# One encoder layer on one core: value and recurrence-input projections moved ahead of the head groups and made token-major, groups cut from 12 to 10 tiles

## The reference

```python
xn = rmsnorm(x, norm_pre_w)
h = xn @ w_in                                   # 2048 x 13312
na_q, na_k, na_v, na_z, hg_q, hg_ff, hg_fb, hg_i, hg_z, gate_pre = split(h)
o_a = neighbourhood_attention(na_q, na_k, na_v, bias) * silu(na_z)      # 16 heads of 64
f, key = lb + (1 - lb) * sigmoid(f_pre), (1 - lb) * sigmoid(-f_pre)     # per direction
# recurrence, forward and backward, 8 heads of 128:
#   S_t = diag(f_t) S_{t-1} + key_t outer i_t ;  o_t = S_t^T q_t
o_b = rmsnorm(o_fwd + o_bwd, hg_norm_w) * silu(hg_z)
g_a, g_b = split(sigmoid(gate_pre + b_gate))
y = g_a * (o_a @ w_branch[:1024]) + g_b * (o_b @ w_branch[1024:])
out = x + rmsnorm(y @ w_out, norm_post_w)
```

## Time and profile before

| | us |
|---|---|
| median of 3 runs | 861.09 (859.41 to 861.10) |
| profiled execution, its own time | 860.94 |
| its span, first to last instruction | 859.2 |
| PE busy | 841.3 (98%) |
| DVE busy | 636.9 (74%) |
| ACT busy | 404.2 (47%) |
| POOL busy | 46.6 (5%) |
| DMA, all queues | 153.44 MB, mean 179 GB/s |

### The profile page before, as it was taken

The page is one execution under the profiler, slowest core; times in us unless marked ns, Lnnn a source line. Parts: engine busy times, 40 slices in busy tenths (PEclk is TensorE's granted clock), DMA queues, the critical chain, the costliest instruction groups (busy, mean ns, idle before and its releaser), DMA issues.

```text
span 859.2 us, 14528 instructions
## 1 busy us (share of the span) xinstructions
PE 841.3 (98%) x4913; PEld 730.7 (85%) x4913; DVE 636.9 (74%) x1304; ACT 404.2 (47%) x667; POOL 46.6 (5%) x51
## 2 busy tenths in 40 slices
PE   6999999999999999999999999999999999999995
PEld 5888888888888888888888888888888888888884
DVE  4877876886888688688878868876875777774444
ACT  6554444435444453644544454345444555554442
POOL 5300000000100000010000001000000000000002
PEclk9999999999999999999999999999999999999998
DMA  9967658565675766666566666656566866576522
GB/s 287 239 183 190 170 148 206 154 191 151 169 191 147 180 180 165 177 164 176 162 167 183 160 181 157 172 164 175 157 186 165 226 185 178 180 275 213 190 100 99
DMA packets 270966, 153.44 MB, mean 179 GB/s; under 512 B 15240, under 2 KB 261088, under 8 KB 270304
## 3 DMA queue, kind: packets, MB, share of 16 engines
q1 hardware_dynamic: 269936, 149.17, 63.5%
q10 hardware_dynamic: 1008, 3.98, 1.2%
HBM read 151.04 MB, written 2.10 MB: 178 GB/s over the span
## 4 chain that ended last, share of the span: by engine, by line
PE 96%; DMA 1%; DVE 1%; ACT 1%; POOL 0%; DVEq 0%; issue 0%; SPq 0%; ACTq 0%
PE psum L960 52%; PE psum L962 26%; PE psum L1034 3%; PE psum L1155 3%; PE psum L1157 3%; PE psum L1156 3%; DMA raw<-in_w_in 1%; PE psum L1020 1%; PE psum L1009 1%; PE psum L989 1%; PE psum L1047 1%; PE psum L1039 0%; PE psum L998 0%; PE psum L1054 0%; ACT w_hi L387 0%; DVE big L922 0%
## 5 line engine op out<-in xcount | busy, mean ns | idle before, releaser
L960 PE MATMUL psum<-act_hl,w_hi 128*128 128x512 f32 x1664 | 593.2, 400 | 0.0
L962 PE MATMUL psum<-act_hl,w_lo 128*128 128x256 f32 x1664 | 463.9, 279 | 0.0
L597 DVE TENSOR_TENSOR w_lo<-raw,w_hi 128x1024 fp32r<-128x1024 f32 x270 | 328.0, 1254 | 75.6 <-ACT w_hi L387 75.1
L960 PEld LDWEIGHTS psum<-act_hl,w_hi 128*128 128x128 f32 x1664 | 312.3, 188 | 73.2 <-DVE w_lo L597 3.1
L962 PEld LDWEIGHTS psum<-act_hl,w_lo 128*128 128x128 f32 x1664 | 313.7, 189 | 0.0
L387 ACT ACTIVATE w_hi<-raw 128x1024 fp32r<-128x1024 f32 x272 | 272.8, 1051 | 30.8 <-PE psum L1157 25.7
L398 ACT ACTIVATE part<-psum 128x256 f32<-128x256 f32 x104 | 39.6, 381 | 261.1 <-PE psum L962 261.1
L960 PE MATMUL psum<-branch_hl,w_hi 128*128 128x512 f32 x256 | 90.7, 399 | 0.0
L962 PE MATMUL psum<-branch_hl,w_lo 128*128 128x256 f32 x256 | 71.9, 281 | 0.0
L960 PEld LDWEIGHTS psum<-branch_hl,w_hi 128*128 128x128 f32 x256 | 48.1, 188 | 12.2 <-DVE branch_hl L763 0.3
L657 DVE TENSOR_TENSOR hg<-hg 128x128 f32<-128x128 f32 x224 | 50.7, 288 | 0.3
(11 more groups left out here) (124 smaller groups left out, 543.3 us busy)
## 6 DMA issues: line engine op xcount, KB each, us to landing
raw<-in_w_in SPq DMA_DIRECT2D x104, 1024.0 KB, 5.7
raw<-in_w_branch SPq DMA_DIRECT2D x16, 1024.0 KB, 6.0
raw<-in_w_out SPq DMA_DIRECT2D x16, 1024.0 KB, 5.1
bias_t<-in_na_rel_bias SPq DMA_DIRECT2D x32, 96.0 KB, 5.7
big<-in_x SPq DMA_DIRECT2D x2, 1024.0 KB, 6.3
big<-in_x ACTq DMA_DIRECT2D x2, 1024.0 KB, 6.8
out<-big SPq DMA_DIRECT2D x5, 256.0 KB, 2.7
wide<-in_norm_post_w ACTq DMA_DIRECT2D x1, 1024.0 KB, 4.7
```

What stands on the lines that cost most here:

```text
L597: nc.vector.tensor_tensor(w_lo[:, i, :], raw[:, r, 1024 * h:1024 * (h + 1)], w_hi[:, i, :].bitcast(F32), ALU.subtract).then_inc(lo_ready, 1)
L960: nc.tensor.matmul(sums[h][:, :], w_hi[:, i, w], operand[:, k, :], start=first, stop=False, skip_group_check=True)
L962: ins = nc.tensor.matmul(sums[h][:, 0:T], w_lo[:, i, w], operand[:, k, 0:T], start=False, stop=last, skip_group_check=True)
```

## The change

1. Value (v) and recurrence input (i) of all heads leave the groups. They are projected first, in 16 tiles of the token-major shape of stage 4 (`early_tile`), 4 blocks of 4 tiles, from x that is transposed unscaled. The result of a block is scaled by the root mean square when ACT copies it out (`take_block`) to the places in `big` that gates take later. Groups have 10 slots; no transposes of v and i; ACT copies v and i of a group to `v_now` and `i_now`.
2. x is loaded in column halves, the weight tiles 0 and 1 between them, tile 0 in two halves. The warm-up matmuls no longer wait for x; there are 12 instead of 16.
3. The scaled `act_hl` is made beside tiles 6 to 14: DVE adds the parts of x and multiplies by the scale (`scale_pair`), ACT makes the high part (`act_hi`), DVE the low part (`act_lo`).
4. The four multiplications of `grow` and of `decayed` become two each, on 256 columns, with an address pattern that goes from one side's tile to the other's and back (`sides`).
5. Steps of a group have other slots; the loop's body is two groups. `hgrn_sum` writes its own bank.
6. At the end DVE weighs the output sums in PSUM in place, and the last scaling reads PSUM instead of SBUF.

```diff
-IN_SLOTS = 12
+IN_SLOTS = 10
+PRE_BLOCKS = 4
+N_PRE = 4 * PRE_BLOCKS
-WARM_UP = 16
+WARM_UP = 12
...
+            load_x(0)
+            early(0)
+            early(1)
+            load_x(1)
+            for n in range(2, N_PRE):
+                early(n)
...
+            for h in range(2):
+                x_hi(2 * h)
+                x_hi(2 * h + 1)
+                split_hi(0, 0, 0, h)
+            for k in range(4, 8):
+                x_hi(k)
+            split_tile(*early_place(1))
+            square(0)
+            for h in range(2):
+                split_hi(*early_place(2), h)
+                x_hi(8 + 2 * h)
+                x_hi(9 + 2 * h)
+            for k in range(12, 16):
+                x_hi(k)
+            square(1)
+            for n in range(2, N_PRE):
+                split_tile(*early_place(n + 1))
+                if n % 4 == 0:
+                    take_block(n // 4 - 1)
...
+                if 6 <= n < 14:
+                    act_hi(n - 6)
...
             def grow(half):
-                for i, (dst, side, src) in enumerate((
-                        (suf_f, 0, bc(pre_f, 1, half - 1)), (pre_b, 1, bc(suf_b, 0, 0)),
-                        (pre_f, 1, bc(pre_f, 0, half - 1)), (suf_b, 0, bc(suf_b, 1, 0)))):
...
+                hg_s.done(nc.vector.tensor_tensor(sides(suf_f, pre_b, half), sides(suf_f, pre_b, half),
+                                                  sides(pre_f, suf_b, half, 2 * half - 1, 0, 0), ALU.mult))
+                hg_s.settle(dve)
+                hg_s.done(nc.vector.tensor_tensor(sides(suf_b, pre_f, half), sides(suf_b, pre_f, half),
+                                                  sides(suf_b, pre_f, half, half, half - 1, 0), ALU.mult))
...
+                if 7 <= n < 15:
+                    act_lo(n - 7)
+                if 6 <= n < 14:
+                    scale_pair(n - 6)
...
-                nc.vector.tensor_tensor(block_columns(o_tok[:, t, :], c), at(psum, c * 2 + t),
+                nc.vector.tensor_tensor(at(psum, c * 2 + t), at(psum, c * 2 + t),
...
+            def early_tile(n):
+
+                c, r = n // 4, n % 4
+                for h in range(2):
+                    if (n, h) == (1, 1):
+                        turn_x(1)
...
+                    if c == 0:
+                        pe.wait_ge(xn_ready, 4 * r + 2 * h + 2)
+                    elif c > 1 and r == 0 and h == 0:
+                        pe.wait_ge(block_taken, 2 * (c - 1))
+                    pe.wait_ge(lo_ready, n * 2 + h + 1)
+                    i = (2 * r + h) % HALVES
                     for t in range(2):
+                        sums = bank[4 + 2 * (c % 2) + t]
+                        for kk in range(2):
...
+                            nc.tensor.matmul(sums, hi, w_hi[:, i, w], start=(k == 0), stop=False)
+                            nc.tensor.matmul(sums, hi, w_lo[:, i, w], start=False, stop=False)
+                            ins = nc.tensor.matmul(sums, lo, w_hi[:, i, w], start=False, stop=(k == KT - 1))
+                    ins.then_inc(half_used, 1)
```

More of the change, by code:

```diff
@@ L157, in encoder_layer @@
         ps_heads = (ps_s, ps_pt)
-        turn_bank = bank[5:8] + bank[0:4] + bank[5:6]
+        turn_bank = bank[0:4] + bank[6:8] + bank[0:2]
+        rstd_rows = ps_o
+        x_hl = branch_hl
+        squares = [hg[:, 4 + 4 * t:8 + 4 * t, :].rearrange("p a b -> p (a b)") for t in range(2)]
+        turner = hg[:, 12, :].rearrange("p (t c) -> p t c", t=2)
+        x_pair = (hg[:, 0:2, :], hg[:, 2:4, :])
+        first_landed = [sem(f"first_landed{h}") for h in range(2)]
         raw_landed = [sem(f"raw_landed{i}") for i in range(RAW)]
@@ L236, in column @@
             return ap[:, i:i + 1] if isinstance(i, int) else ap[:, bass.ds(i, 1)]
-        def pairs(ap, half):
-            return ap.rearrange("p (n two h) -> p n two h", two=2, h=half)
         def both_tiles(ap):
@@ L282, in _ @@
+            load_x(0)
[4 more added lines that the diff above has]
+                early(n)
+            for p in range(2):
+                group(0, p)
+            with loop(sp, 2, NG - 1, 2) as g0:
+                for p in range(2):
+                    group(g0, p)
             for t in range(TAIL):
-                col = GATE_TILE + 3 * NG + t
-                load(t % RAW, w_in_v[:, :, col * P:col * P + P], tile_no(NG, t))
+                col = GATE_TILE + TAIL_GATES[t]
+                n, r, _ = place(NG, 0, t)
+                load(r, w_in_v[:, :, col * P:col * P + P], n)
@@ L513, in _ @@
+            group(0, 0, True)
+            group(0, 1, False)
+            with loop(act, 2, NG - 1, 2) as g0:
+                for p in range(2):
+                    group(g0, p, False)
             for t in range(TAIL):
-                n = tile_no(NG, t)
-                split_next(n, n // RAW, n % RAW)
+                split_tile(*place(NG, 0, t + 1))
                 if t > 0:
-                    gate_tanh(3 * NG + t - 1, n - 1)
+                    gate_tanh(TAIL_GATES[t - 1], NG, t - 1)
@@ new lines, in rstd_set_up, with make_turner @@
+            def rstd_set_up():
+                dve.wait_ge(ss_ready, 4)
+                link(nc.vector.tensor_tensor(ssum, ssq[:, 0:2], ssq[:, 2:4], ALU.add))
+                nc.vector.tensor_scalar(msq, ssum, 1.0 / D, EPS, ALU.mult, ALU.add).then_inc(msq_ready, 1)
+            def make_turner():
+                dve.wait_ge(rstd_ready, 1)
+                dve.wait_ge(const_step, 5)
+                for t in range(2):
+                    nc.vector.tensor_scalar(turner[:, t, :], block[:, 0, :], rstd[:, t:t + 1], None,
+                                            ALU.mult).then_inc(turner_ready, 1)
@@ L856, in _ @@
+            group(0, 0, True)
+            group(0, 1, False)
+            with loop(dve, 2, NG - 1, 2) as g0:
+                for p in range(2):
+                    group(g0, p, False)
             for t in range(TAIL):
-                n = tile_no(NG, t)
-                split_next(n, n % RAW)
+                split_tile(*place(NG, 0, t + 1)[0:2])
                 previous(NG, t)
-                take_tile(n, t % 2, gates[:, 3 * NG + t, :])
+                take_tile(NG, t, gates[:, TAIL_GATES[t], :])
@@ L1091, in previous, with group @@
                     turn_rst(g - 1)
-            def group(g, first):
+            def group(g0, p, first):
+                g = g0 + p
                 for s in range(IN_SLOTS):
-                    n = tile_no(g, s)
-                    wait(pe, tile_out, n - 1)
+                    n, r, _ = place(g0, p, s)
+                    wait(pe, tile_out, made(g, s - 2))
                     def between():
```

499 lines of the change are left out of this document (269 added, 230 removed).

## The result

The changed kernel takes 854.0 us (median of 4 runs, 853.1 to 856.2) against 860.9 of before (859.4 to 861.1): ratio 0.9927, 95% interval 0.9915 to 0.994. That is 0.7% faster, where 1.5% was forecast. Forecast and time are 6.2 us apart. The profiled execution is the slowest of the four, 856.16 us for a span of 854.4; the others have spans of 851.4 to 852.3. The sum of the prediction was 846.1 of span, so 8.3 us of that trace have to be found.

The account below looks back on a forecast made before the run. PE was taken to bound the kernel. From a span of 859.2, 7.6 us (early stage), 3.7 (transposes of v and i) and 1.8 (end) leave 846.1; plus 1.74 outside the span, 847.8 us, range 844.5 to 856.

Parts of the forecast that it names:

- the start: Before the early tiles: vectors there by 5.9 us, first projection matmul at 10.4, 6.2 us earlier than before.
- The chain behind the vectors: Before the early tiles: first bank full at 7.1 us, ACT's copies and both halves, then first matmul at 10.4.
- the pace after it: First early tiles: matmuls as fast as the same form in the output projection, 227 ns each.
- rival (a): Early stage gives most gain back: late vectors or slow PE pace (2.2 us), the circle 2.5 more; 850 to 854, chance 0.22.
- the circle: Tiles 6 to 15: ACT and DVE wait on each other, 6.1 us a turn against PE's 5.44; PE waits 1.2 us.
- the form: Sixteen early tiles: token-major takes 5.44 us a tile against 5.655 feature-major, 3.4 us less in all.
- Groups: Groups of 10 tiles instead of 12: 64.2 us of PE instead of 76.0, nothing added to the path.
- i's transposes: In the groups: taken at 0.23 us like v's; dropping both saves 3.7 us in all.
- 5.655 us of a tile: Pitch of a feature-major tile, two of which were subtracted from each group's 76.0 us.
- DVE had room: In the groups: DVE busy 51.1 of 64.2 us, with 30 merged level operations at 0.36 each.
- Rival (b): DVE bounds the groups; merged operations at 0.68 us would make 868 us, deciding from about 0.65 a piece; chance 0.10.
- The end: After the last matmul: DVE's three additions take 2.1 us instead of 4.08; 1.8 us less for the whole.

Follow-up runs that it names:

- e11: Changed kernel with all of SP's loads held back until the four vector loads have landed: 856.0 us, one run.
- e12: Changed kernel with x's left halves loaded at once but the weights held back until the four vector loads have landed: 855.5 us, one run.
- e2: Changed kernel with x's left half transposed ahead of the small vectors: 852.1 us, ratio 0.9903 to the kernel before.
- e9: As e7, but 24 warm-up pieces instead of 36 and 28 filler pieces instead of 30: 849.1 us, ratio 0.9877 to the kernel before.
- e1: Changed kernel with 22 warm-up matmuls instead of 12 and 14 unread ones after x's first transposes: 852.5 us, ratio 0.9909 to the kernel before.
- e6: Changed kernel with the old unmerged `grow` and `decayed`, eight operations in place of four: 854.6 us, ratio 0.9925 to the kernel before.
- e8: Changed kernel run once more, unchanged: 854.2 us, ratio 0.9929 to the kernel before.
- e4: Changed kernel with the recurrence level put ahead of the heads' outputs in slot 7: 854.1 us, ratio 0.9931 to the kernel before.
- e5: Kernel before with only part 6 of the change (output sums weighed in PSUM, last scaling reads PSUM): 859.9 us, ratio 0.9988.
- e7: Changed kernel with x transposed first, 36 warm-up pieces, 30 filler pieces, and e3's order: 850.8 us, ratio 0.989 to the kernel before.
- e3: Changed kernel with DVE's multiplication by the scale ahead of the next tile's low halves: 852.2 us, ratio 0.9913 to the kernel before.
- e10: e7's kernel again, unchanged, beside e9: 851.4 us, ratio 0.9901 to the kernel before.

## Why the prediction was half right

**Wrong: the start.** The step that failed is "The vectors (norm weights) must be there by 5.9 too"; of the last of them it says itself that "the trace doesn't show when it lands". From it the first matmul was put at 10.4. In the changed kernel they land at 8.2, behind the traffic (e11, e12). The trace of before does date them, against that sentence: the last 26 of the 144 packets of their queue pass between 7 and 8 us there (none between 8 and 9), so they landed at 7 to 8 us. That queue in the kernel before, from 7 to 8 us (packets, MB, share of the engines):

```profile
q10 hardware_dynamic: 26, 0.00, 2.2%
```

The chain behind the vectors was forecast rightly: from the first full bank to the first matmul 3.3 us in the sum (7.1 to 10.4), and from ACT's first copy on 3.2 in the trace (10.11 to 13.29). With x transposed first (e2, e9) what remains of this error is 12.1 against 10.4, 1.7 us.

**Wrong: the pace after it.** "Its cost could differ only if the early matmuls were slower than the same form in the output projection, and I know no reason for it". The reason was named in rival (a) and priced at 2.2; it came to 2.9 (e1). It was argued away with one pause of 1.4 us in the earlier trace rows behind which the transposes ran at full pace. Here PE had two pauses, 2.06 and 2.01 us, and the granted clock read 0.50 from 10 to 18 us. The argument went from one pause to a rule. Rival (a), 850 to 854 us with a chance of 0.22, is what happened, at its upper edge, by both halves of its first condition (late vectors and the slow pace); its other part, 2.5 us more from the circle, did not.

**Right: the form.** 24 matmuls take 5.44 us in the early tiles too: behind the slow stretch they follow each other by 0.23 (21.01, 21.24, 21.47 in the timeline), and nothing but the slow stretch and the one wait is added. e9's tile 16, 89.35 us after its first matmul, is 16 x 5.44 = 87.0, 1.84 and 0.36 for transposes, and 0.1.

**The circle: right in its turn, lucky in its wait.** 6.1 us a turn were forecast and 5.93 measured; the lead at the start of the circle was 4.3 us forecast and 4.2 measured. By that a tile loses 0.5 and not 0.7, and the lead lasts: without the mask beside the multiplication PE does not wait (e6, e8). The wait of 1.1 us in this trace against 1.2 forecast is luck, since it needs 1.7 us of DVE beside POOL's mask, which the sum did not have.

**Groups: a tile's price was mis-sized.** The group is 64.38 us instead of 64.2, with PE never waiting for DVE. It is not the level operations (e6) and not the weight load behind the heads' outputs (e4). Nor is it i's transposes, taken by analogy with v's at 0.23: in before the level's matmuls start 0.22 behind them. It is the 5.655 us of a tile, read in the branch projection and used for tiles of the groups. In the groups 16 pairs of matmuls take mostly 16 x 0.3467 = 5.55 us; over the whole group of before, in which about a quarter of the pairs go at 0.353, it is 5.57. In the timeline of before, 30 pairs without a step between them, and i's transposes:

```profile
195.85 0.40 PE L960 MATMUL psum<-act_hl,w_hi 128*128 128x512 f32 x1
...
206.25 0.40 PE L960 MATMUL psum<-act_hl,w_hi 128*128 128x512 f32 x1
...
226.81 0.38 PE L998 MATMUL psum<-block,hg 128*128 128x128 f32 x2
227.03 0.61 PE L1034 MATMUL psum<-q_dec,k_dec 128*128 128x128 f32 x4
```

With it a group is 76.0 - 2 x 5.57 - 2 x 0.22 = 64.42, and 15 tiles at 0.085 less make 1.3 of the 1.7 us. The other 0.4 stay open.

DVE had room, as forecast: 53.90 busy of 64.38 instead of 51.1, of which 30 merged operations at 0.42 instead of 0.36 are 1.8. Rival (b), 868 us, needed 0.65 a piece. By the Trainium skill (Vector Engine (DVE) Microarchitecture Reference, 5.2 Measured stream behaviour on trn2) an operation whose tiles alternate at every word costs about twice the usual time an element (0.58 us in the prediction's estimate), and those with longer runs nothing more. The trace agrees within a tenth: L738's seven in that group have a mean of 449 ns with a median of 419 and a highest of 632, so one of the seven takes 0.63. With L741's highest, 646, and the products of level 0 at 0.49 it is 0.6 us a group, against an estimate of 0.8. All of it is hidden.

**The end.** 1.8 forecast, 1.1 measured (e5 alone 1.1 too). DVE's three additions are 2.07, forecast at 2.1, and the last addition, now POOL's (2.93 went to 2.49), ends 2.0 us nearer to the last matmul. The term that was missing is the outputs behind the additions: the sum left their time as it was, and it rose by 1.0 us (e5).

**The profile and the runs.** 854.4 of span is the longest of the four executions. How long the slow stretch lasts varies: 13 slow matmuls in this trace, 7 in e8's of the same kernel, which has no wait at tile 15 either. The size of the error by the runs is 6.2 us.

## What to carry to other kernels

When loads are moved ahead or reordered, give each small one that gates the start a landing time of its own; issued at 2 us beside megabytes of other traffic, it may land at 8. Where the start is made of short waits of PE, fill them with matmuls nobody reads (e1, and e9 against the changed kernel), but no longer than the wait, since every piece too many delays what is ready (e7 against e9). At the end of a kernel, sum up to the last output and not to the last operation: additions that ended 2.0 us earlier brought the end 1.1 us nearer. And take the price of a tile from the stage in which it lies: 0.085 us a tile were 1.3 us in all.

## What the runs showed of the hardware that was not expected

- The same instructions meet a different clock at the start from one execution to the next. With a pause of PE of 2.0 to 4.1 us before the first tile, matmuls of the first tiles ran at the slow pace in seven of eight traces (the changed kernel, e3, e4, e6, e8, e11, e12), and not in e2's, with 3.50 us of pause. In e8, the changed kernel once more, the clock fell twice and was at 1.00 between. Its busy time by stretch, with the granted clock third from the end:

```profile
8.00:10.00 2.00, 1.59 (x8) 1.62 (x9) 0.00 (x0) 0.24 (x1) 1.57 (x6) 0.55 1.05 407
...
12.00:14.00 2.00, 0.00 (x0) 0.00 (x0) 2.00 (x4) 2.00 (x4) 0.00 (x0) 1.00 1.02 407
...
16.00:18.00 2.00, 2.00 (x6) 1.51 (x6) 2.00 (x5) 2.00 (x3) 0.00 (x0) 0.50 1.06 389
```

- The branch projection, 256 pairs of matmuls of 512 and 256 columns, has two paces, 90.66 or 89.01 us from first to last, at the same granted clock and with no wait. The groups' pairs show the same two paces, 0.347 and 0.353 us. Two traces of one kernel, e7 and e10, show one each. The first and the last matmul of the stage in e7 (in e10 they start at 662.80 and 753.47):

```profile
662.61 0.48 PE L1084 MATMUL psum<-branch_hl,w_hi 128*128 128x512 f32 x1
...
751.62 0.28 PE L1086 MATMUL psum<-branch_hl,w_lo 128*128 128x256 f32 x1
```

  The 1.65 us are about the distance between the two levels of the kernel before (859.2 and 860.9) and of e9 (848.9 and 850.7). The traces of before and of the changed kernel both have 90.66, so it is no part of the difference between them, but it hides an effect of 1 us in a single run: e9's trace has a span 0.5 us longer than e7's, though all of its early stage is 1.1 us ahead.
- A DVE operation with two SBUF inputs took 2.34 us instead of 0.68 while POOL worked on 128 x 768 elements (e3's section), and the three last additions, with one input in PSUM, took 2.07 beside POOL instead of 4.08 (e5). In the changed kernel it ended at 97.58, and POOL's at 97.03 (94.69 + 2.34): as if it had got through only behind it. In the traces here the one that starts first decides: in e8 and e6, 0.13 and 0.17 us ahead of POOL's, the same operation took 0.68 and 0.69. The Trainium skill (SBUF — State Buffer, Who interferes with whom) says that a DVE instruction with two SBUF inputs contends with a GpSimd instruction that reads SBUF, and calls the contention an exclusive lock; these rows agree.
